# Expert outputs added to a table of sums in DRAM by accumulating indirect transfers

## The chip, the cores and the metric

The kernel runs on one core of a Trainium2 chip. The core has a matrix engine (TensorE, PE in the profile), a vector engine (VectorE, DVE), a scalar engine (ScalarE, ACT), a general engine (GpSimd, POOL) that also issues the indirect transfers, and a queue engine (SyncE, SP) that issues most loads. Sixteen DMA engines move data for all the queues. The metric is the device time of one execution in microseconds (us); less is better.

## The reference, cut to what matters

Two trunk layers run over 640 tokens: 512 latent tokens and 128 context ("prompt") tokens. Each layer ends with an expert-choice mixture of experts. There are 16 experts. Each expert picks its 64 best latent tokens and its 16 best prompt tokens, runs a gated network of width 1024 on these 80 rows, weighs each row by the router's number, and adds it to the row of its token:

```
cap = CAPACITY_FACTOR * n_tok // N_EXPERTS
g, idx = lax.top_k(aff.T, cap)
xe = xt[idx]
hid = jax.nn.silu(jnp.einsum('ecd,edf->ecf', xe, w1)) * jnp.einsum('ecd,edf->ecf', xe, w3)
ye = jnp.einsum('ecf,efd->ecd', hid, w2) * g[..., None].astype(h.dtype)
out = jnp.zeros_like(xt).at[idx.reshape(-1)].add(ye.reshape(-1, D))
...
x = x + gate2 * expert_choice_ffn(h, p['w_router'], p['w_ff1'], p['w_ff3'], p['w_ff2'])
```

The weights are in fp32: three matrices of 1024 x 1024 for each expert, 12 MB. One token can be picked by several experts, so the last line is a sum that several experts write to.

## The kernel before, in words

**State.** The residual stream `x` lies in SBUF with the model dimension on the partitions: 8 tiles of 128 x 640 tokens. Everything that an expert produces has tokens on the partitions, so it has to be spread over tokens and turned before it can be added to `x`.

**A pair of experts.** The experts are worked in 8 pairs (A and B) for each layer. SP streams a pair's weights as 24 chunks of 1 MB into a ring of six buffers (line 705, `ring<-in_w_ff`). It issues a chunk once POOL has counted its buffer free (`chunks_free`, helper `release`). A chunk is two units. For each unit ACT rounds the weights (`w_hi`, `hi_of_chunk`, line 1415), DVE makes the rest (`w_lo`, `lo_of_chunk`, line 1839), and PE multiplies (`job`, line 1361, six matmuls of 512 columns). There are four `w_hi` and four `w_lo` buffers, so ACT and DVE can be four units ahead of PE. A pair has six jobs of eight units: AF0, AF1, BF0, BF1 (hidden halves of A and B), AO and BO (outputs of A and B), 48 units or 288 matmuls. Between them PE turns the hidden values (line 1373) and the next pair's tokens (line 1320), which POOL has fetched from the table `h_rows` in DRAM by indirect transfers (`fetch`, line 770).

**Outputs before.** After job AO, and again after BO, `outputs` of ACT copies the 16 prompt rows from PSUM, makes the rounded and weighed 64 latent rows (`ye_hi`), and issues a store of the prompt rows to DRAM (line 1788). `outputs` of DVE makes the rest (`ye_lo`, line 1847). The latent rows of A lie on partitions 0 to 63 and those of B on 64 to 127; for that B's tokens are padded to 128 rows (`ROWS_OF`, `LAT_OF`). DVE also builds `hot_t`, a 128 x 512 matrix with a one where slot meets token (`place`).

**Combine before.** In the next pair, ahead of each of the eight units 8 to 15 (job AF1), PE multiplies one eighth of `ye_lo` and of `ye_hi` by `hot_t` into a bank of its own (`combine`, line 1331, two matmuls of 512 columns), and DVE adds the result to `x` (`spread`, line 1847). The first pair has nothing to combine. After the last pair the eight combines run by themselves, and then the prompt rows of all 16 experts are read back and multiplied in the same manner (`combine_p`, line 1396), and eight additions end the layer.

**Order.** Each engine's program is written out by hand in this order; engines meet at semaphores. The counts in the loops (`n == 5 + 4 * q`, `n == 21` and so on) say behind which chunk of the pair a step stands on its engine. Pair 0 and the last pair are written out, the six between are a loop.

## Time and profile before

| what | value |
|---|---|
| median of 3 runs | 3278.09 us (3276.85 to 3278.34) |
| the profiled execution | 3273.44 us, its span 3271.7 us |
| granted TensorE clock, mean | 0.948 |
| PE, DVE, ACT, POOL busy | 90%, 65%, 48%, 2% of the span |
| data moved | 566.97 MB, mean 173 GB/s |

All rows quoted below come from one profiled execution, with times in us from the start of its span. "Busy" counts the time in which an engine works on an instruction; matmuls are pipelined, so that one matmul lasts 0.39 us while the next starts 0.23 us after it. The distance from start to start is therefore the better measure of what a matmul costs. The DMA share is the busy share of the 16 DMA engines; it can read a little over 1.

### The profile page before, as it was taken

What the parts mean: (1) busy time and instruction counts of PE and PEld (TensorE: products, weight loads), DVE (VectorE), ACT (ScalarE), POOL (GpSimd) and SP (SyncE); (2) the same over time, 40 slices, a digit from 0 to 9 for tenths busy, and PEclk for the clock granted to TensorE, in tenths of its full rate; (3) what the DMA queues carried; (4) which work ended last, traced back from release to release, by engine and by line L of the source; (5) the groups of instructions that cost most, each with busy time, mean ns of one, the idle gap of its engine ahead of it and who ended that gap; (6) DMA issues with size and microseconds to landing.
All of it is one profiled execution on the core that took longest, in us unless ns stands there. A gap on an engine that the chain in (4) does not pass through costs nothing.

```text
span 3271.7 us, 42479 instructions
## 1 busy us (share of the span) xinstructions
PE 2939.5 (90%) x14740; PEld 2070.8 (63%) x14740; DVE 2114.8 (65%) x3030; ACT 1574.3 (48%) x2328; POOL 58.4 (2%) x86
## 2 busy tenths in 40 slices
PE   5988989999977999999978899889999599999994
PEld 2666755667644776667636677557775366777763
DVE  3274445466445999999844653446662699999994
ACT  3162244124124777777732613431510387777773
POOL 0000000000001000000000000000000000000000
PEclk8998999899987999999989899999999799999996
DMA  7102100310228999999921202020112499999991
GB/s 278 52 33 103 64 27 27 104 67 1 110 77 309 359 345 343 341 338 330 334 84 58 78 34 81 2 104 27 67 39 97 161 361 343 338 344 344 342 338 49
DMA packets 285039, 566.97 MB, mean 173 GB/s; under 512 B 18824, under 2 KB 24672, under 8 KB 284256
## 3 DMA queue, kind: packets, MB, share of 16 engines
q1 hardware_dynamic: 276416, 538.39, 46.3%
q10 hardware_dynamic: 5024, 16.16, 1.3%
q0 software_dynamic: 3456, 10.50, 1.2%
q8 instruction: 92, 1.51, 0.2%
q14 instruction: 51, 0.42, 0.0%
HBM read 548.32 MB, written 16.68 MB: 173 GB/s over the span
## 4 chain that ended last, share of the span: by engine, by line
PE 74%; ACT 8%; DVE 7%; issue 4%; ACTq 3%; DMA 3%; DVEq 1%; POOL 0%; POOLq 0%; SPq 0%
PE mm L1361 24%; PE mm L869 14%; PE mm L827 12%; PE mm L871 4%; DVE w_lo L1839 3%; PE mm L1113 2%; PE mm L899 2%; ACT w_hi L1415 2%; PE oo L1331 2%; ACTq L1787 1%; PE oo L1133 1%; PE tp L1121 1%; PE mm L1201 1%; ACT pt L1415 1%; PE mm L922 1%
## 5 line engine op out<-in xcount | busy, mean ns | idle before, releaser
L1839 DVE TENSOR_TENSOR w_lo<-ring,w_hi 128x1024 fp32r<-128x1024 f32 x768 | 909.7, 1221 | 68.1 <-ACT w_hi L1415 48.7
L1415 ACT ACTIVATE w_hi<-ring 128x1024 fp32r<-128x1024 f32 x768 | 802.7, 1059 | 267.5 <-PE mm L1361 242.7
L1415 ACT ACTIVATE dw_hi<-ring 128x512 fp32r<-128x512 f32 (+1 forms) x168 | 104.9, 627 | 646.6 <-PE mm L871 618.2
L1839 DVE TENSOR_TENSOR dw_lo<-ring,dw_hi 128x512 fp32r<-128x512 f32 (+1 forms) x168 | 115.2, 689 | 399.9 <-ACT dw_hi L1415 399.8
L869 PE MATMUL mm<-h_hi,dw_lo 128*128 128x512 f32 (+1 forms) x672 | 326.4, 486 | 12.1 <-issue 6.2
L871 PEld LDWEIGHTS mm<-h,ring 128*128 128x128 f32 (+1 forms) x1344 | 254.9, 190 | 60.7
L869 PE MATMUL mm<-h_hi,dw_hi 128*128 128x512 f32 (+1 forms) x672 | 268.4, 399 | 0.0
L869 PE MATMUL mm<-h_lo,dw_hi 128*128 128x512 f32 (+1 forms) x672 | 266.5, 397 | 0.0
L827 PE MATMUL mm<-scratch,ring 128*128 128x512 f32 (+1 forms) x896 | 257.9, 440 | 1.6 <-ACT scratch L1415 1.6
L871 PE MATMUL mm<-h,ring 128*128 128x128 f32 (+1 forms) x1344 | 259.1, 274 | 0.0
L827 PEld LDWEIGHTS mm<-scratch,ring 128*128 128x128 f32 x896 | 142.5, 194 | 112.1 <-issue 109.6
L1361 PE MATMUL mm<-w_lo,xa_hi 128*80 128x512 f32 x512 | 204.1, 399 | 9.8 <-DVE w_lo L1839 9.8
L1361 PE MATMUL mm<-w_lo,hid_hi 128*128 128x512 f32 (+1 forms) x512 | 205.9, 402 | 3.2 <-DVE w_lo L1839 2.5
L1361 PE MATMUL mm<-w_lo,xb_hi 128*128 128x512 f32 x512 | 202.5, 396 | 0.0
L1361 PE MATMUL mm<-w_hi,xa_lo 128*80 128x512 f32 x512 | 202.1, 395 | 0.0
L1907 DVE RECIPROCAL tmp<-tmp 128x640 f32<-128x640 f32 x48 | 199.3, 4153 | 3.5
L1361 PE MATMUL mm<-w_hi,hid_lo 128*128 128x512 f32 (+1 forms) x512 | 201.4, 393 | 0.0
L1361 PE MATMUL mm<-w_hi,hid_hi 128*128 128x512 f32 (+1 forms) x512 | 201.0, 393 | 0.0
L1361 PE MATMUL mm<-w_hi,xa_hi 128*80 128x512 f32 x512 | 200.8, 392 | 0.0
L1361 PE MATMUL mm<-w_hi,xb_hi 128*128 128x512 f32 x512 | 199.7, 390 | 0.0
L1361 PE MATMUL mm<-w_hi,xb_lo 128*128 128x512 f32 x512 | 199.3, 389 | 0.0
L1415 ACT ACTIVATE scratch<-mm 128x512 f32<-128x512 f32 (+4 forms) x144 | 97.8, 691 | 158.3 <-PE mm L922 46.3
(255 smaller groups left out, 4631.5 us busy)
## 6 DMA issues: line engine op xcount, KB each, us to landing
ring<-in_w_ff SPq DMA_DIRECT2D x384, 1024.0 KB, 5.9
ring<-in_w_ada SPq DMA_DIRECT2D x48, 1024.0 KB, 7.9
ring<-in_w_gate SPq DMA_DIRECT2D x24, 1024.0 KB, 7.4
ring<-in_w_in SPq DMA_DIRECT2D x16, 1024.0 KB, 10.2
ring<-in_w_o SPq DMA_DIRECT2D x8, 1024.0 KB, 8.7
x_spill<-x ACTq DMA_DIRECT2D x2, 2560.0 KB, 8.6
h_rows<-merged ACTq DMA_DIRECT2D x10, 512.0 KB, 2.7
ring<-in_w_br_da SPq DMA_DIRECT2D x4, 1024.0 KB, 14.2
```

Source lines behind the costliest of these rows:

```text
L827: last = pe.matmul(out[:, lo:hi], lhs(n), rhs(n)[:, lo:hi], start=(n == 0), stop=(n == terms - 1))
L869: pe.matmul(out[0:width, 0:NLAT], w_[u % 2][:, kk, 0:width], h_[:, k, 0:NLAT], start=(k == 0 and i == 0), stop=(k == KT - 1 and i == 2))
L871: last = pe.matmul(out[0:width, NLAT:T], weight(chunk, k, c0, c0 + width), h[:, k, NLAT:T], start=(k == 0), stop=(k == KT - 1))
L899: last = pe.matmul(mm[j % 2][:, 0:width], h[:, k, t * P:(t + 1) * P], weight(chunk, k, c0, c0 + width), start=(k == 0), stop=(k == KT - 1))
L922: last = pe.matmul(mm[turn % 2][32 * kk:32 * kk + 32, 0:512], c_cols[:, half * HALF + kk, :], ring[g % RING][:, kk, :], start=(half == 0), ...
L1113: last = pe.matmul(mm[j % 2][:, at:at + hi - lo], ml_q[hd % 2][:, t * P:(t + 1) * P], ml_k[hd % 2][:, lo:hi], start=True, stop=True)
L1121: last = pe.transpose(tp[:, b * P:(b + 1) * P], ml_p[i % 3][:, b * P:(b + 1) * P], ident)
L1331: last = pe.matmul(oo[j % 2][:, :], y[:, k * P:(k + 1) * P], hot_t[:, :], start=(i == 0), stop=(i == 1))
L1361: last = pe.matmul(out[0:rows_, bank:bank + 512], a_[:, k, 0:rows_], b_[n % SPLITS][:, kk, :], start=(k == 0 and i == 0), stop=(k == KT - ...
L1415: return act.activation(out, in_, ACT.Copy, scale=scale)
L1839: return dve.tensor_tensor(out, in0, in1, op)
L1907: dve.reciprocal(t_[:, :], t_[:, :])
```

## The change

The sum over experts moves from PE and DVE to the DMA engines. Two tables `sums` of 640 x 1024 in DRAM, one for each layer, are set to zero by ten stores early in the first layer (POOL, from a zeroed row tile of `merged`). After AO and after BO, ACT copies all 80 rows of the expert, weighed, from PSUM into a plain fp32 buffer (`ye`), and POOL issues an indirect transfer that adds these 80 rows of 4 KB to the rows of their tokens in `sums` (`add`). The additions are ordered: each waits until the one before it has landed (`added`). They stand behind the release of chunk 22 (for A) and of chunk 3 of the next pair (for B); the token fetches move from chunks 3 and 6 to 4 and 7. At the layer's end ACT waits for the last addition, loads the whole table (2.5 MB) into `merged`, PE turns it in 40 transposes, and DVE adds it to `x` in 16 instructions.

Gone are: `hot_t`, `ye_hi` and `ye_lo`, the combines and their additions, the stores of prompt rows with their read-back and product, the small transfers of `slot_p`, and the padding of B to 128 rows (all jobs now work on 80 rows).

The core of the diff:

```
-PAIR_MM, PAIR_T, PAIR_O = 6, 6, 8
+PAIR_MM, PAIR_T = 6, 6
-        x_hi = [rounded("xa_hi", "scratch", 6144, [P, KT, CAP]), rounded("xb_hi", "scratch", 7424, [P, KT, P])]
+        x_hi = [rounded("xa_hi", "scratch", 6144, [P, KT, CAP]), rounded("xb_hi", "scratch", 7424, [P, KT, CAP])]
-        ye_hi = rounded("ye_hi", "scratch", 11520, [P, D])
-        ye_lo = rounded("ye_lo", "pt", 0, [P, D])
+        ye = [view(11520, D), view(12544, D)]
...
+        def added_count(l, e, half):
+            return 16 * (DEPTH * TT + 2 * l * PAIRS + half) + 32 * e
...  POOL
+            pool.wait_ge(t_full, T_BEFORE)
+            pool.memset(tok[:, 0, :], 0.0).then_inc(zero_ready, 1)
+                if l == 0:
+                    pool.wait_ge(zero_ready, 1)
+                    for n in range(DEPTH):
+                        for t in range(TT):
+                            pool.dma_start(a["sums"][n][t * P:(t + 1) * P, :], tok[:, 0, :]).then_inc(added, 16)
+                def add(of, half):
+                    pool.tensor_copy(row_to[0:CAP, half:half + 1].bitcast(U32),
+                                     row_no[0:CAP, bass.ds(2 * of + half, 1)].bitcast(U32)).then_inc(row_to_ready, 1)
+                    pool.wait_ge(ye_ready, 2 * (l * PAIRS + of) + (half + 1))
+                    pool.wait_ge(added, added_count(l, of, half))
+                    pool.sem_inc(pool_waited, 1)
+                    pool.drain()
+                    pool.indirect_dma_start(a["sums"][l],
+                                            bass.IndirectOffsetOnAxis(ap=row_to[0:CAP, half:half + 1].bitcast(U32), axis=0),
+                                            ye[half][0:CAP, :], None, compute_op=ALU.add).then_inc(added, 16)
+                def pair(e, before=None, last_pair=False):
                     for n in range(PAIR_CHUNKS):
                         release(e, n)
-                        if n in (3, 6):
+                        if n == 3 and before is not None:
+                            add(before, 1)
+                        if n in (4, 7) and not last_pair:
                             ...
                             fetch(e + 1, half)
+                        if n == 22:
+                            add(e, 0)
...  PE
-                        if before is not None and COMBINE_AT <= n < COMBINE_AT + KT:
-                            combine(n - COMBINE_AT, before)
-                                last = pe.matmul(out[0:rows_, bank:bank + 512], a_[:, k, 0:rows_],
+                                last = pe.matmul(out[0:CAP, bank:bank + 512], a_[:, k, 0:CAP],
-                for k in range(KT):
-                    combine(k, PAIRS - 1)
+                pe.wait_ge(ye_back, l * 16 + 16)
+                for k in range(KT):
+                    j = MM["back"] + k
+                    wait_mm_empty(pe, l, j)
+                    for t in range(TT):
+                        last = pe.transpose(mm[j % 2][:, t * P:(t + 1) * P], tok[:, t, k * P:(k + 1) * P], ident)
+                    last.then_inc(mm_full[j % 2], 1)
...  ACT
+                    act.wait_ge(added, added_count(l, e, half) - 16)
+                    copy(ye[half][0:CAP, :], mm[j % 2][0:CAP, :], aff_now[0:CAP, half:half + 1])\
+                        .then_inc(mm_empty[j % 2], 1)
                     act.drain()
-                    act.dma_start(a["ye_pr"][2 * e + half], ye_pr[PR_OF[half], :]).then_inc(ye_stored, 16)
+                    act.sem_inc(ye_ready, 1)
+                act.wait_ge(added, added_count(l, PAIRS, 0))
+                act.dma_start(tok[:, :, :], a["sums"][l].rearrange("(t p) c -> p t c", p=P)).then_inc(ye_back, 16)
...  DVE
+                        if l == 0 and m == 0:
+                            dve.wait_ge(added, 16 * DEPTH * TT)
-                    stt(ye_lo[rows_, :], mm[j % 2][rows_, :], aff_slot[rows_, :], f(ye_hi[rows_, :]),
-                        ALU.mult, ALU.subtract).then_inc(mm_empty[j % 2], 1)
-                            spread(m - SPLITS - COMBINE_AT, before)
+                    j = MM["back"] + k
+                    wait_mm_full(dve, l, j)
+                    for lo, hi, g in groups:
+                        last = stt(x[:, k, lo:hi], mm[j % 2][:, lo:hi], mod[:, 40 + k, g:g + 1], x[:, k, lo:hi],
+                                   ALU.mult, ALU.add)
```

**PE, in the loop over pairs, around units 8 and 9 (job AF1).** Before, two matmuls of the combine stand ahead of each unit (`w_lo_85` and `w_hi_89` are the buffers of unit 8, `oo` the bank of the combine):

```order
2546 L1361 MATMUL mm<-w_hi_92,xa_hi 80x512
2547 L573 ISA
2548 L1331 MATMUL oo<-hot_t,ye_lo 128x512
2549 L1331 MATMUL oo<-hot_t,ye_hi 128x512
2550 L1356 REGISTER_ALU
2551 L1361 MATMUL mm<-w_lo_85,xa_hi 80x512
...
2556 L1361 MATMUL mm<-w_hi_89,xa_hi 80x512
2557 L1331 MATMUL oo<-hot_t,ye_lo 128x512
2558 L1331 MATMUL oo<-hot_t,ye_hi 128x512
```

In the changed kernel the eight pairs of `oo` matmuls are gone, and unit follows unit on the same two banks `mm`.

**PE, at the layer's end.** Before, 16 matmuls of the last combine and 16 of the prompt rows follow the last unit:

```order
3176 L1361 MATMUL mm<-w_hi_92,hid_hi_98 128x512
3177 L1331 MATMUL oo<-hot_t,ye_lo 128x512
...
3192 L1331 MATMUL oo<-hot_t,ye_hi 128x512
3193 L1396 MATMUL mm<-scratch 128x128 x16
3194 L942 MATMUL tp<-const,rows 128x108
```

And in the changed kernel, where 40 transposes of 128 x 128 from the table that was read back (`merged`) take their place:

```order
2846 L1353 MATMUL mm<-w_hi_92,hid_hi_98 80x512
2847 L1383 MATMUL mm<-const,merged 128x128 x40
2848 L948 MATMUL tp<-const,rows 128x108
```

What moved: the sum is no longer formed on PE; what is left there is one turn of the whole table, behind a load.

**POOL, in the loop over pairs.** In the changed kernel (the second number is the line; `sums<-scratch` is an addition, `merged<-h_rows` a fetch, each `REGISTER_ALU` run belongs to the waits and releases of chunks):

```order
25 L774 COPY scratch<-scratch 80x1
26 L776 REGISTER_ALU
27 L777 ISA
28 L780 DMA sums<-scratch 640x1024
...
33 L765 COPY scratch<-scratch 80x1
34 L768 DMA merged<-h_rows,scratch 80x1024
...
38 L765 COPY scratch<-scratch 80x1
39 L768 DMA merged<-h_rows,scratch 80x1024
40 L790 REGISTER_ALU x15
...
45 L780 DMA sums<-scratch 640x1024
```

Before, the loop of this engine held the two fetches alone. Now it holds four indirect transfers for each pair, and the releases of chunks stand behind them in the same queue.

## Rows read from the trace of the kernel before

**Rows 1.** From the page: busy time, share and instructions of each engine.
```profile
PE 2939.5 (90%) x14740; PEld 2070.8 (63%) x14740; DVE 2114.8 (65%) x3030; ACT 1574.3 (48%) x2328; POOL 58.4 (2%) x86
```

**Rows 2.** Windows, core 0: length, busy time by engine, clock, DMA share, GB/s.
```profile
1037.60:1110.10 72.50, 70.83 (x327) 51.28 (x326) 66.34 (x69) 60.61 (x68) 3.63 (x5) 1.00 1.03 365
1186.30:1262.50 76.20, 73.65 (x337) 53.28 (x336) 70.27 (x73) 58.78 (x65) 2.94 (x4) 1.00 0.96 337
```

**Rows 3.** Timeline of PE, starts of units 8 and 16: start, length, instruction.
```profile
1040.02 0.40 PE L1361 MATMUL mm<-w_lo,xa_hi 128*80 128x512 f32 x1
...
1051.35 0.39 PE L1361 MATMUL mm<-w_lo,xb_hi 128*128 128x512 f32 x1
...
1187.52 0.40 PE L1331 MATMUL oo<-hot_t,ye_lo 128*128 128x512 f32 x1
...
1203.60 0.40 PE L1361 MATMUL mm<-w_lo,xb_hi 128*128 128x512 f32 x1
...
1263.73 0.40 PE L1331 MATMUL oo<-hot_t,ye_lo 128*128 128x512 f32 x1
```

**Rows 4.** Timeline of ACT, DVE and PE between two pairs.
```profile
1180.48 1.11 ACT L1415 ACTIVATE ye_hi<-mm,stat 64x1024 fp32r<-64x1024 f32 x1
1182.31 5.08 ACT L1415 ACTIVATE w_hi<-ring 128x1024 fp32r<-128x1024 f32 x5 [0.72 <-issue]
1183.40 6.91 DVE L1839 TENSOR_TENSOR w_lo<-ring,w_hi 128x1024 fp32r<-128x1024 f32 x6 [0.49 <-ACT w_hi L1415]
1184.68 0.46 PE L1361 MATMUL mm<-w_lo,xa_hi 128*80 128x512 f32 x1 [0.70 <-DVE w_lo L1839]
```

**Rows 5.** Timeline of PE: each third matmul of B's input, then of A's output.
```profile
1222.82 0.39 PE L1361 MATMUL mm<-w_lo,xb_hi 128*128 128x512 f32 x1
...
1225.54 0.39 PE L1361 MATMUL mm<-w_lo,xb_hi 128*128 128x512 f32 x1
...
1226.93 0.39 PE L1361 MATMUL mm<-w_lo,hid_hi 128*80 128x512 f32 x1
...
1229.73 0.39 PE L1361 MATMUL mm<-w_lo,hid_hi 128*80 128x512 f32 x1
```

**Rows 6.** The same for 10 us at full rate, and 10 with fetches.
```profile
1060.00:1070.00 10.00, 10.00 (x48) 8.26 (x47) 9.60 (x12) 8.05 (x9) 0.00 (x0) 1.00 1.05 386
1270.00:1280.00 10.00, 10.00 (x48) 6.86 (x47) 9.98 (x13) 5.68 (x7) 1.30 (x2) 1.00 1.05 336
```

**Rows 7.** DMA issues: out and in, queue, count, KB each, median us to landing.
```profile
ring<-in_w_ff SPq DMA_DIRECT2D x384, 1024.0 KB, 5.9
x_spill<-x ACTq DMA_DIRECT2D x2, 2560.0 KB, 8.6
merged<-h_rows,scratch POOLq DMA_INDIRECT x32, 7.5
```

**Rows 8.** Timeline of POOL and PE: the second fetch, one under load, turns.
```profile
1022.98 0.92 POOL L770 DMA_INDIRECT merged<-h_rows,scratch  x1 [2.27 <-issue]
1026.92 1.30 PE L1320 MATMUL tp<-const,merged 80*128 80x80 f32 x8 [3.34 <-DMA merged<-h_rows,scratch]
1187.83 1.00 POOL L770 DMA_INDIRECT merged<-h_rows,scratch  x1 [0.89 <-issue]
1235.62 0.74 PE L1320 MATMUL tp<-const,merged 80*128 80x80 f32 x8 [0.40 <-DVE hid_lo L1839]
```

**Rows 9.** Timeline of the first layer's end, and a turn of eight tiles.
```profile
966.37 1.97 PE L1302 MATMUL tp<-const,h 128*128 128x128 f32 x8 [0.97 <-DVE scratch L2289]
1630.29 0.39 PE L1361 MATMUL mm<-w_hi,hid_hi 128*128 128x512 f32 x1
1640.75 1.41 DVE L1847 SCALAR_TENSOR_TENSOR x<-oo,mod,x 128x512 f32<-128x512 f32 x2 [0.16 <-PE oo L1331]
1646.15 2.16 DVE L1847 SCALAR_TENSOR_TENSOR x<-mm,mod,x 128x128 f32<-128x128 f32 x8 [3.99 <-PE mm L1396]
```

**Rows 10.** Windows: a stretch of attention in the first layer.
```profile
180.00:200.00 20.00, 13.33 (x68) 8.26 (x69) 12.74 (x33) 8.99 (x21) 0.00 (x0) 0.74 0.10 35
```

More of the change, by code:

```diff
@@ L199 @@
     ("pairs", 0)])
-MM["combine_p"] = _mm_dense + PAIRS * PAIR_MM
-MM_LAYER = MM["combine_p"] + 1
+MM["back"] = _mm_dense + PAIRS * PAIR_MM
+MM_LAYER = MM["back"] + KT
 MM_USES = [(MM_LAYER + 1) // 2, MM_LAYER // 2]
@@ L266 @@
 TOKENS_AT = (38, 42)
-COMBINE_AT = JOB_UNITS
 def job_turn(q):
@@ L803, in _ @@
                             fetch(e + 1, half)
-                for n in range(PAIR_CHUNKS):
-                    release(PAIRS - 1, n)
+                        if n == 22:
+                            add(e, 0)
+                pair(0)
+                with pool.Fori(1, PAIRS - 1) as e:
+                    pair(e, e - 1)
+                pair(PAIRS - 1, PAIRS - 2, True)
+                add(PAIRS - 1, 1)
         @block.tensor
@@ L1322, in turn_tokens, with job @@
                     last.then_inc(t_full, 1)
-                def combine(k, of):
-                    if k == 0:
-                        pe.wait_ge(ye_done, l * PAIRS + of + 1)
-                    j = OO["pairs"] + k
-                    wait_o_empty(pe, l, j, of)
-                    for i, y in enumerate((ye_lo, ye_hi)):
-                        last = pe.matmul(oo[j % 2][:, :], y[:, k * P:(k + 1) * P], hot_t[:, :],
-                                         start=(i == 0), stop=(i == 1))
-                    last.then_inc(o_full[j % 2], 1)
-                def job(q, e, before=None, last_pair=False):
+                def job(q, e, last_pair=False):
                     half = q % 2 if q >= AO else q // 2
-                    rows_ = ROWS_OF[half]
                     hi, lo = (hid_hi[half], hid_lo[half]) if q >= AO else (x_hi[half], x_lo[half])
@@ L2310, in _ @@
                 dve.tensor_copy(row_no[0:CAP, :].bitcast(U32), tp[0:CAP, 0:NE]).then_inc(slots_ready, 1)
[L2311 to L2317 removed]
+                dve.tensor_copy(slot_aff[0:CAP, :], tp[0:CAP, NE:2 * NE]).then_inc(t_empty, 1)
                 dve.drain()
@@ L2401, in pair @@
                         if n == 14:
-                            place(e)
-                        if n == 21:
-                            if not last_pair:
-                                lo_of_tokens(0, e + 1)
-                            outputs(AO, e)
+                            weigh(e)
+                        if n == 21 and not last_pair:
+                            lo_of_tokens(0, e + 1)
                         if n == 23 and not last_pair:
@@ L2413, in _ @@
                     lo_of_tokens(half, 0)
-                pair(0)
-                place_prompt()
-                with dve.Fori(1, PAIRS - 1) as e:
-                    pair(e, e - 1)
-                pair(PAIRS - 1, PAIRS - 2, True)
-                outputs(BO, PAIRS - 1)
-                for k in range(KT):
-                    spread(k, PAIRS - 1)
-                dve.drain()
-                j = MM["combine_p"]
-                wait_mm_full(dve, l, j)
-                for k in range(KT):
-                    stt(x[:, k, NLAT:T], mm[j % 2][:, k * P:(k + 1) * P], mod[:, 40 + k, 1:2], x[:, k, NLAT:T],
-                        ALU.mult, ALU.add)
-                dve.drain()
-                for s in (mm_empty[j % 2], x_ready, layer_free):
+                with dve.Fori(0, PAIRS - 1) as e:
+                    pair(e)
+                pair(PAIRS - 1, True)
+                for k in range(KT):
+                    j = MM["back"] + k
[3 more added lines that the diff above has]
+                                   ALU.mult, ALU.add)
+                    last.then_inc(mm_empty[j % 2], 1)
+                dve.drain()
+                for s in (x_ready, layer_free):
                     dve.sem_inc(s, 1)
@@ L2469 @@
     a["h_rows"] = nc.dram_tensor("h_rows", (T, D), FP32, kind="Internal").ap()
-    a["slot_p"] = nc.dram_tensor("slot_p", (2, SLOTS_P), FP32, kind="Internal").ap()
-    a["ye_pr"] = nc.dram_tensor("ye_pr_rows", (NE, CAP_P, D), FP32, kind="Internal").ap()
+    a["sums"] = [nc.dram_tensor(f"sums{n}", (T, D), FP32, kind="Internal").ap() for n in range(DEPTH)]
     build(nc, a)
```

151 lines of the change are left out of this document (35 added, 116 removed).

## The prediction

> **What bounds the kernel now.** I read the page first. PE is busy for 90% of the span, DVE for 65% and POOL for 2% [rows 1]. The change touches the expert stages, so I then asked for windows of one pair each. A pair in the loop lasts 76.2 us. PE is busy for 73.65 of them at clock 1.00, DVE for 70.3 and ACT for 58.8, and the DMA share is 0.96 at 337 GB/s [rows 2]. So three resources are close together, and PE is the one that paces: its matmuls follow each other at 0.23 us and it waits little. Third I read the timelines of PE: where the combines stand, what happens between two pairs, and what a matmul on 80 rows costs [rows 3 to 5]. Fourth, since the change gives work to the DMA engines, I looked for their ceiling. There are windows of 10 us at 386 GB/s with the share at 1.05 [rows 6]. Last I read the end of the layer, where PE and DVE finish what the stage left over [rows 9].
>
> **PE in the stage: less by 32.6 us a layer.** Three terms.
> - The combines. Pair 0 has none: its units 8 to 15 take from 1040.02 to 1051.35, 11.33 us. In a pair that has them the same units take from 1187.52 to 1203.60, 16.08 us [rows 3]. That is 4.75 us for 16 matmuls of 0.23 (3.7) and the stalls on the two `oo` banks. Seven pairs of a layer have them: 33.3 us. The eighth set stands in the tail, below.
> - The boundary. ACT makes the prompt copy and `ye_hi`, issues a store, and resumes `w_hi` at 1182.31; DVE resumes `w_lo` at 1183.40, and PE waits 0.70 us for it [rows 4]. Afterwards one copy of 80 x 1024 (like the 1.11 us of `ye_hi`) and no `ye_lo` stand there, so both resume more than 1 us sooner and the wait goes: 7 x 0.7 = 4.9 us.
> - The padding of B. Matmuls on 128 rows start 2.72 us apart for twelve, those on 80 rows 2.80 for twelve [rows 5]. In a pair 96 input matmuls of B and 48 output matmuls go from 128 rows to 80. The output ones cost 4 x 0.08 = 0.3 us by these rows. Units 8 to 15 of pair 0, on 80 rows, took 11.33 us for 48 matmuls and four small transposes (0.2), so 0.231 each against 0.227: 0.4 us for 96. I take 0.7 us a pair, which costs 8 x 0.7 = 5.6 us. Fewer rows save nothing, because 512 columns stream either way.
>
> Sum: -33.3 - 4.9 + 5.6 = -32.6 us a layer. If PE still paces, the stage that ended at 1630.5 [rows 9] ends at 1597.9, and a pair lasts about 71.5 us. DVE loses its additions and `ye_lo` (some 8 us of a pair) and ACT a copy, so neither takes PE's place.
>
> **DMA in the stage: does it still keep up?** This decides the case. At 386 GB/s a chunk of 1.049 MB takes 2.72 us. From the first free buffer (a ring of six is full at the start) 186 chunks have to come: 505 us. A fetch moves 0.33 MB, 0.85 us at that rate; but with fetches in flight the share stays 1.05 and the rate falls to 336 GB/s, which costs 10 x 50 / 386 = 1.3 us more [rows 6]; I take 2.0 us each, 14 of them: 28 us. With the small stores the need is 536 us. By the other measure, share over the saturated 1.05, the stage of 602 us needs 0.91 of itself, 550 us [rows 2]; the share overstates a queue that isn't full. I take 540, of which 2.5 go with the stores of prompt rows.
>
> An addition appears in no row. Bounds: 0.85 us if it costs no more than its bytes, and 15 us if each DMA engine takes its 5 rows one after the other and is held for 3 us by each, which is what an unloaded fetch takes from the end of its issue to its landing (1022.98 + 0.92 to 1026.92) [rows 8]. The nearest row is the fetch, 2.0 us, to which an addition adds one more passage over the same bytes (read the table, read `ye`, write the table): 2.0 + 0.85 = 2.85 us. Fifteen of them before the last chunk: 43 us.
>
> The last chunk then lands at 1029 + 537.5 + 43 = 1609.5, and after it come one `w_hi` (1.1), one `w_lo` (1.2) and two units of six matmuls (2.8): 1614.6. That is later than PE's 1597.9, so the DMA engines pace the stage. It ends 16 us sooner than before, and not 33.
>
> The Trainium skill ("DMA: Bandwidth & Descriptors", section Specifications) speaks against the change: HBM gives one core about 358 GB/s. The trace has stretches of 386 GB/s [rows 6], so the rule doesn't hold for this kernel as it runs; taken literally it would make the chunks alone last 545 us and the changed stage end some 40 us later than in my sum.
>
> **POOL.** Its queue holds the releases of chunks. An addition costs it a small copy, a drain of 0.9 us and 1.0 us of issue [rows 8], 2.5 us in all, and the next release is due 2.8 us later: it fits. The wait for `ye_ready` is over before it is asked, since ACT makes the copy ahead of the `w_hi` on which the release of chunk 22, or chunk 3, depends. The wait for the addition before is over if that landed within the five chunks (14 us) between; fetches land in 7.5 [rows 7]. Were it late, chunks behind it would be released late, and SP would wait: that is part of rival 2. The zeroing writes 5.2 MB (14 us at full rate) where the DMA share is 0.10, long before `merged` is written [rows 10]: nothing. The iota, the `slot_p` transfers and the small DVE copies ahead of the stage: -0.3 us.
>
> **The tail: more by about 10.5 us a layer.** Before, from the last matmul's start at 1630.29 to the end of the last addition at 1648.31 [rows 9]: 17.8 us after the product is there. Now: ACT's copy 1.1 and drain 0.2; POOL 1.0 and issue; landing about 4.5 from the issue's start (the unloaded fetch: 3.9); then the load of 2.5 MB, 8.6 as the spill of the same size [rows 7]. PE starts at about +15.2. A transpose of 128 x 128 takes 1.97 / 8 = 0.246 us [rows 9], 40 of them 9.85; DVE works beside them (0.71 + 0.27 = 0.98 for each five) and ends 1.2 later. PE has been idle for 15 us, and the trace shows what that does: the same eight small transposes take 1.30 us when PE was idle ahead of them and 0.74 in the stream [rows 8]; I add 2 us for it. Sum 28.3, more by 10.5. Bounds: +7 (landing 3, clock back at once) to +20 (the addition lands in 14 us).
>
> **Sum.** Per layer -16 + 10.5 = -5.5 and the small -0.3, so -11.6 for two. The profiled execution took 3273.4 us (span 3271.7), so 3261.8; the median of the runs stands 4.7 above the profiled one: 3266.5.
>
> **Rivals.**
> 1. PE still paces, because an addition costs 1.7 us or less. For: additions are spread thinly, and in rows 2 the rate of 365 GB/s was held over a whole pair. Against: a fetch already costs 2.0. Per layer -32.6 + 10.5 - 0.3 = -22.4: 3233 us.
> 2. Slower: an addition costs more than a plain transfer, because each row is read, added and written back by an engine that the weight loads need. The loss begins at 537.5 + 15c + 5.1 + 1029.3 + 10.2 = 1630.5, which is c = 3.2 us. At 5 us the two layers lose 2 x 15 x 1.8 = 54: 3332. At 15 us, 3632. For: nothing hides it, the DMA share is already 0.96. Against: only the bound from serial rows makes it dear.
> 3. The stage gains what I say, but the gain and the tail cancel (c of 2.9 to 3.3, or a landing of 14 us): 3272 to 3284.
> 4. The change does what it says only on paper: POOL falls behind and holds the releases. Each late release costs its lateness; 2 us a pair make 32 us: about 3300. For: four indirect transfers a pair in the queue that frees the ring; against: the 2.8 us between releases.
> 5. Memory as a whole caps the rate, reads and writes together, at the 365 GB/s that pair 0 kept up as its mean [rows 2]. A chunk then takes 2.87 us, 28 us more for 186: 3323. Against: 386 GB/s for 10 us at a time [rows 6]. The skill's 358 GB/s is a rule of this kind; it has its chance here.
>
> **Chances.** Forecast (DMA paces, additions 1.7 to 2.9 us, 3233 to 3271): 0.36. Rival 1: 0.17. Rival 3: 0.14. Rival 2: 0.23. Rival 4: 0.07. Rival 5: 0.03. Within 0.2% (6.6 us), about what a measurement of this kernel can tell, lies rival 3. Faster: 0.36 + 0.17 = 0.53; same 0.14; slower 0.33. The forecast's own range is 3233 to 3271; my value of an addition lies at its upper end. The range that should hold 8 in 10 reaches to rival 1 on one side and to an addition of 5 us on the other: 3230 to 3332.
>
> **What would show it.** Right: the pairs last 73 to 75 us, all alike but for the first; ACT's `w_hi` waits for the landing of `ring<-in_w_ff`, the median landing of which rises from 5.9 us to over 9; the share is 1.03 or more through the stage; the last matmul to the end of the layer takes about 28 us. PE pacing would show as pairs of 71.5 us and `w_hi` waiting for PE. Rival 2: pairs over 76 us with GB/s below 340 at full share. Rival 4: SP waits for POOL while POOL waits for `sums<-scratch`. I am wrong as a whole if units 8 to 15 don't shrink to 11.3 us, or if the tail grows by less than 5 or more than 20 us.

## The result, and the profile after

| | median | runs | ratio to before |
|---|---|---|---|
| before, on the same chip | 3277.47 us (3275.89 to 3278.34) | 4 | |
| changed | 3226.28 us (3223.72 to 3226.98) | 4 | 0.984, 95% interval 0.983 to 0.986 |

I predicted 3267 us, within 3230 to 3332. The kernel became 51 us faster and the time lies below the range. What came out is rival 1: PE still paces, 3233 us by its sum. The profiled execution took 3226.98 us, its span 3225.1 us, 46.6 us less than before.

The page after, to be held against [rows 1]: PE lost 58 us of work and POOL gained 102.

```profile
PE 2881.5 (89%) x14500; PEld 1938.4 (60%) x14500; DVE 1993.6 (62%) x2820; ACT 1531.8 (47%) x2264; POOL 160.8 (5%) x147
```

Windows of the changed kernel (length, busy time by engine, clock, DMA share, GB/s), for [rows 2]. Each has the length of one pair: the first begins in the third pair of layer one, the other at the end of the fifth.

```profile
1187.53:1257.40 69.87, 69.23 (x321) 44.62 (x320) 62.67 (x60) 56.65 (x62) 10.21 (x9) 1.00 1.05 375
1382.09:1452.69 70.60, 69.38 (x322) 44.49 (x321) 62.18 (x60) 55.69 (x61) 10.07 (x8) 1.00 1.05 375
```

From first matmul to first matmul, the second and third pair last 69.9 us and the later ones 70.4 to 70.6, where it was 76.2. PE is busy for all but 0.6 us of the early stretch. The share is 1.05, that of the windows at full rate in [rows 6].

Starts of units 0, 8, 16, 32 and of the next pair's unit 0 on PE, for [rows 3]. Before, unit 8 started with a combine and unit 16 came 16.08 us later.

```profile
1176.74 0.39 PE L1353 MATMUL mm<-w_lo,xa_hi 128*80 128x512 f32 x1
...
1187.77 0.40 PE L1353 MATMUL mm<-w_lo,xa_hi 128*80 128x512 f32 x1
...
1199.12 0.40 PE L1353 MATMUL mm<-w_lo,xb_hi 128*80 128x512 f32 x1
...
1221.83 0.40 PE L1353 MATMUL mm<-w_lo,hid_hi 128*80 128x512 f32 x1
...
1246.61 0.39 PE L1353 MATMUL mm<-w_lo,xa_hi 128*80 128x512 f32 x1
```

And those of the kernel before that [rows 3] don't have: unit 0, B's input to its end, and the pair's end.

```profile
1175.54 0.40 PE L1361 MATMUL mm<-w_lo,xa_hi 128*80 128x512 f32 x1
...
1226.22 0.40 PE L1361 MATMUL mm<-w_lo,hid_hi 128*80 128x512 f32 x1
...
1251.77 0.40 PE L1361 MATMUL mm<-w_lo,xa_hi 128*80 128x512 f32 x1
```

Unit 0 to 8 took 11.98 us and takes 11.03; units 8 to 15 took 16.08 and take 11.35. Job B's input, 96 matmuls, takes 22.71 us on 80 rows and took 22.62 on 128 (from 1203.60). The two output jobs took 25.55 and take 24.78. The boundary between the pairs on ACT and DVE, for [rows 4]: one copy, then `w_hi` again, and no wait of PE.

```profile
1180.66 1.10 ACT L1401 ACTIVATE scratch<-mm,scratch 80x1024 f32<-80x1024 f32 x1
1181.99 3.00 ACT L1401 ACTIVATE w_hi<-ring 128x1024 fp32r<-128x1024 f32 x3 [0.23 <-issue]
...
1183.09 7.20 DVE L1819 TENSOR_TENSOR w_lo<-ring,w_hi 128x1024 fp32r<-128x1024 f32 x6 [1.07 <-ACT w_hi L1401]
```

POOL in the fifth pair (start, length, instruction, idle before). The addition of the pair before (1327.79) is followed by a fetch, and between the fetch's small copy and its issue POOL stands idle for 5.5 us:

```profile
1327.79 1.51 POOL L780 DMA_INDIRECT sums<-scratch  x1 [0.91 <-issue]
1328.83 1.75 POOL L765 COPY scratch<-scratch 80x1 uint32 x1
1336.12 1.07 POOL L768 DMA_INDIRECT merged<-h_rows,scratch  x1 [5.54 <-issue]
```

What ACT waited for from 1311.45 to 1382.09, a pair's length (engine, operand, line, releaser: us in total, times, longest):

```profile
ACT w_hi L1401 <- PE mm L1353: 8.0, 20, 1.6
ACT w_hi L1401 <- DMA ring<-in_w_ff: 6.3, 9, 1.4
```

DMA queues in three windows of 10 us of the changed kernel (queue, packets, MB, busy share of the 16 engines): one with nothing but chunks, one with a single addition, one with a single fetch. q1 are the chunks, q0 POOL's transfers.

```profile
q1 hardware_dynamic: 1938, 3.87, 105.2%
...
q1 hardware_dynamic: 1674, 3.33, 89.0%
q0 software_dynamic: 96, 0.33, 16.4%
...
q1 hardware_dynamic: 1682, 3.35, 94.1%
q0 software_dynamic: 96, 0.33, 10.9%
```

An addition takes 0.54 MB of chunks away from its window, which is 1.40 us at 387 GB/s. A fetch takes 0.52 MB, 1.34 us. The other windows of this kind in the stage read the same: 3.32 or 3.33 MB of chunks beside nearly every addition, 3.33 to 3.38 beside most fetches.

The start of a stage, for [rows 8]: the second fetch is issued at 1026.77 and PE turns its rows at 1033.95, 7.2 us later; before it was 3.9.

```profile
1026.77 0.95 POOL L768 DMA_INDIRECT merged<-h_rows,scratch  x1 [3.76 <-issue]
...
1033.95 1.30 PE L1326 MATMUL tp<-const,merged 80*128 80x80 f32 x8 [6.96 <-DMA merged<-h_rows,scratch]
```

The end of the first layer, for [rows 9]: an addition, the last matmul, the last addition, the load of the table, the turns, and DVE's last group of additions into `x`.

```profile
1593.30 1.55 POOL L780 DMA_INDIRECT sums<-scratch  x1 [0.86 <-issue]
...
1596.35 0.39 PE L1353 MATMUL mm<-w_hi,hid_hi 128*80 128x512 f32 x1
...
1601.74 1.43 POOL L780 DMA_INDIRECT sums<-scratch  x1 [6.70 <-DMA sums<-scratch]
...
1609.19 0.39 ACTq L1801 DMA_DIRECT2D merged<-sums  x1
...
1618.20 5.63 PE L1383 MATMUL mm<-const,merged 128*128 128x128 f32 x25 [21.47 <-DMA merged<-sums]
...
1622.01 5.82 DVE L1827 SCALAR_TENSOR_TENSOR x<-mm,mod,x 128x512 f32<-128x512 f32 x12 [0.36 <-PE mm L1383]
```

From the last matmul's start to the end (1627.83) it is 31.5 us, before 18.0. In layer two it is 27.1 us against 17.6. There the last addition is issued 2.9 us after the last matmul's start, and not 5.4, and it lands in 5.2 us (the load is issued at 3158.49), and not in 7.5. What differs is the traffic beside it. In layer one SP has already issued six loads of 1 MB for the next layer (`ring<-in_w_in`, from 1585.47 on), and the last layer has no next one. The addition in layer two, and the two stretches from issue to landing, layer one first (the two last columns are DMA share and GB/s):

```profile
3153.31 1.43 POOL L780 DMA_INDIRECT sums<-scratch  x1 [4.21 <-DMA sums<-scratch]
```

```profile
1601.74:1609.19 7.45, 0.00 (x0) 0.00 (x0) 0.00 (x0) 0.00 (x0) 1.43 (x1) 0.50 0.89 293
3153.31:3158.49 5.18, 0.00 (x0) 0.00 (x0) 0.00 (x0) 0.00 (x0) 1.43 (x1) 0.72 0.46 63
```

So the span's 46.6 us are: the two stages, first matmul to start of the last, -41.0 and -40.9; the two ends +13.5 and +9.5; from the first fetch's issue to the stage's first matmul +3.9 and +3.1 (9.83 to 13.70 us, 13.36 to 16.45). That is -51.9. The rest, +5.3, lies in the dense parts; +3.2 of it is there when the first fetch is issued, and executions of the changed kernel differ by 2.4 us at that point.

### The profile page after: what moved, and what is told of

Its sections match the earlier page's. It is cut to its first block, busy times and chain, and to the rows that moved or that the text cites. A ratio compares the mean times of both kernels' runs of the same rounds, so it can differ in the third digit from the quotient of the medians.

```text
span 3225.1 us, 41854 instructions
## 1 busy us (share of the span) xinstructions
PE 2881.5 (89%) x14500; PEld 1938.4 (60%) x14500; DVE 1993.6 (62%) x2820; ACT 1531.8 (47%) x2264; POOL 160.8 (5%) x147
## 4 chain that ended last, share of the span: by engine, by line
PE 70%; DMA 10%; DVE 6%; issue 6%; ACT 5%; ACTq 1%; POOLq 1%; DVEq 1%; POOL 0%; SPq 0%
PE mm L1353 19%; PE mm L875 15%; PE mm L833 12%; DMA ring<-in_w_ff 6%; PE mm L877 5%; PE mm L1119 2%; PE mm L905 2%; DVE w_lo L1819 2%; ACT w_hi L1401 1%; PE oo L1139 1%; PE tp L1127 1%; PE mm L1207 1%; PE mm L1010 1%; PE mm L928 1%; PE tp L1219 1%
## 5 line engine op out<-in xcount | busy, mean ns | idle before, releaser
L1353 PE MATMUL mm<-w_lo,hid_hi 128*80 128x512 f32 x512 | 204.3, 399 | 0.0
L1353 PE MATMUL mm<-w_lo,xb_hi 128*80 128x512 f32 x512 | 203.0, 396 | 0.0
L1353 PE MATMUL mm<-w_hi,hid_hi 128*80 128x512 f32 x512 | 202.3, 395 | 0.0
L1353 PE MATMUL mm<-w_hi,hid_lo 128*80 128x512 f32 x512 | 202.3, 395 | 0.0
L1353 PE MATMUL mm<-w_hi,xb_lo 128*80 128x512 f32 x512 | 201.7, 394 | 0.0
L1353 PE MATMUL mm<-w_hi,xb_hi 128*80 128x512 f32 x512 | 200.2, 391 | 0.0
L875 PEld LDWEIGHTS mm<-h_hi,dw_hi 128*128 128x128 f32 (+1 forms) x672 | 128.0, 190 | 30.0
```

Source lines behind the costliest of these rows:

```text
L875: pe.matmul(out[0:width, 0:NLAT], w_[u % 2][:, kk, 0:width], h_[:, k, 0:NLAT], start=(k == 0 and i == 0), stop=(k == KT - 1 and i == 2))
L1353: last = pe.matmul(out[0:CAP, bank:bank + 512], a_[:, k, 0:CAP], b_[n % SPLITS][:, kk, :], start=(k == 0 and i == 0), stop=(k == KT - 1 an ...
```

## The experiments

All are compared with the kernel before on their own chip, whose median was 3276.7 to 3278.1 in the four sets of runs. "Stage" is the first layer's, from its first matmul to the start of its last: 602.3 us before, 561.4 in the changed kernel. Its end is counted from there to DVE's last addition.

### 1. No additions

```
-                            add(before, 1)
...
-                            add(e, 0)
...
-                act.wait_ge(added, added_count(l, PAIRS, 0))
+                act.wait_ge(added, 16 * DEPTH * TT)
```

> The changed kernel with all 32 additions left out (the table stays zero, so the experts' outputs do not reach the result), and with the waits for them. Theory A (PE paces the changed stage, the DMA engines only just keep up): pairs of 69.5 to 70.6 us, at most 1 us less than the 70.6 of the changed kernel, so the two stages shrink by 0 to 16 us in all; the end of the layer loses the landing of the last two additions, some 12 us a layer. Time 3185 to 3204. Theory B, the step of my prediction (the DMA engines pace the changed stage and an addition costs them 2.85 us): 15 of them come before the last chunk of a stage, so the stage would fall by 43 us until PE holds it; PE was then faster than I counted, pairs of about 66 us and a time near 3130.

Measured: 3202.46 us, ratio 0.977 (0.976 to 0.979). Stage 558.6 us. Theory A holds: 16 additions cost the stage 2.8 us in all. Theory B is dead. Of the 24 us between this kernel and the changed one, 15 lie at the layers' ends, where two landings are gone (23.5 us for 31.5, and 20.4 for 27.1; I had expected 12 a layer), and 6 in the two stages. A stretch of one pair's length:

```profile
1258.72:1328.56 69.84, 69.20 (x321) 44.63 (x320) 62.66 (x60) 56.63 (x62) 4.23 (x5) 1.00 1.04 370
```

PE has 69.20 of 69.84 us, so this is PE's own pace.

### 2. Two more additions in each pair, and six

```
+                        if n in (11, 15) and before is not None:
+                            i = (11, 15).index(n)
+                            again(before, i % 2, i // 2)
```

`again` issues the same transfer into a further table (`sums_x`), behind a wait for the last one into that table and a drain of its own. There are two such tables, taken in turn.

> The changed kernel with two more additions in each pair but the first, of the same rows into two further tables, between chunks 11 and 15, where the POOL queue is free. The profile of the changed kernel shows 1.64 us of the 16 engines for the packets of one addition. Theory A (the engines are full at 1.05 in the changed stage, an addition costs 1.6 us of them): pairs go from 70.6 to 73 to 74 us, 14 x 2.4 to 3.4 = 34 to 48 us more in all: 3260 to 3275. Theory B (2.85 us each): 14 x 5.7 = 80 us more: 3306. Theory C (there is slack, PE alone paces): pairs stay under 71.5, 3226 to 3240.

> The same with six more additions in each pair but the first, at chunks 9, 11, 13, 15, 17 and 19. Against the kernel with two more, the slope gives the price of one without regard to who paces at the start: 4 x 14 = 56 additions. Theory A, 1.64 us each: 92 us over the kernel with two more, pairs of 80 us. Theory B, 2.85 us: 160 us over it, pairs of 85 us. Rival: the POOL queue, which an addition holds for some 2 us, comes to hold the releases of chunks; then SP waits for POOL and the DMA share falls below 1.0.

Measured with two more: 3261.06 us, ratio 0.996 (0.994 to 0.997), stage 579.5. That is 18.1 us for 14 additions in the stage, 1.3 each: theory A, whose 1.6 is the nearer value. With six more: 3536.36 us, ratio 1.079 (1.077 to 1.081), stage 722.4. That is 143 us for 28 further ones, 5.1 each, and 275 us in both layers, where theory A had 92 and theory B 160: the rival took over. A stretch of one pair's length, what SP waited for in it, and POOL's transfers:

```profile
1289.87:1382.53 92.66, 74.63 (x321) 47.01 (x320) 62.43 (x60) 55.90 (x62) 17.40 (x14) 0.89 0.94 307
```

```profile
SPq L697 <- POOLq L804: 79.6, 14, 8.8
```

```profile
1340.86 1.68 POOL L793 DMA_INDIRECT sums_x<-scratch  x1 [7.35 <-DVE w_lo L1836]
1350.61 1.41 POOL L793 DMA_INDIRECT sums_x<-scratch  x1 [8.06 <-issue]
```

The share falls to 0.94 and the rate to 307 GB/s: the DMA engines have room and don't get the work. SP waits for POOL for 79.6 us of 92.7. POOL brings out one indirect transfer in about 9 us, since the drain ahead of each waits for the one before; ten of them are the pair's 92.7 us. This is rival 4 of the prediction. It bounds a pair with eight additions, and not yet one with four.

### 3. Is it the adding? Plain writes

```
-                                            ye[half][0:CAP, :], None, compute_op=ALU.add).then_inc(added, 16)
+                                            ye[half][0:CAP, :], None).then_inc(added, 16)
```

> The changed kernel with its 32 transfers into the table as plain indirect writes instead of additions (a row then holds only the last expert's output). Theory A (adding costs the DMA engines more than writing, since the row of the table is read too): the packets of one transfer fall from the 1.64 us of 16 engines that the profile of the changed kernel shows to the 1.1 us of a fetch, ACT waits less for the chunks, pairs of 70.0 instead of 70.6 us, time 8 to 12 us less: 3214 to 3218. Theory B (the price is that of the packets' way, not of the adding): 1.64 us as before, no change: 3226. In both the landing of the last two stays near 7.5 us.

Measured: 3211.79 us, ratio 0.980 (0.978 to 0.982). Theory A, a little more than it said. A window of 10 us with one write in it, to be held against the one with an addition above:

```profile
q1 hardware_dynamic: 1799, 3.59, 96.8%
q0 software_dynamic: 96, 0.33, 8.2%
```

A write occupies the 16 engines for 8.2% of 10 us, an addition for 16.4%: 0.82 and 1.64 us, exactly twice. It takes 0.28 MB of chunks away, 0.7 us, half of an addition's 1.4. The stage is 558.7 us and ACT waits for no chunk. The last transfer also lands sooner, which neither theory had: in 5.3 us instead of 7.5, in layer two in 3.3 instead of 5.2. The end is 28.0 instead of 31.5 us, in layer two 24.7 instead of 27.1.

### 4. POOL's hold, or the DMA engines? One addition moved

```
-                        if n == 3 and before is not None:
+                        if n == 12 and before is not None:
                             add(before, 1)
```

> The changed kernel with the addition of the pair before's second half (BO) issued behind chunk 12 and not behind chunk 3. In the changed kernel the fetch behind chunk 4 follows that addition, and POOL's drain ahead of it waits 5.6 us, in which no release of a chunk can go out; ACT then waits for ring<-in_w_ff. Theory A (the 0.3 us a pair that the kernel without additions was faster come from POOL's hold): the wait goes, pairs shrink from 70.2 to 69.9, 5 us less in all: 3221. Theory B (they come from the engines' own work for an addition, twice that of a plain write): no change, 3226.

> The changed kernel itself, unchanged, for a comparison on the same chip with the two others: 3226, between 3222 and 3229.

Measured: 3218.24 us moved, ratio 0.9825 (0.9812 to 0.9839), and 3221.56 us for the changed kernel again, 0.9833 (0.9819 to 0.9846), a little below the 3222 to 3229 that I had said. The two medians differ by 3.3 us and the intervals overlap, so by the times it is a hint. The stages are clearer: 558.7 against 561.5, and 557.8 against 560.8 in layer two. ACT's waits in four pairs, of the changed kernel again and then of the moved one:

```profile
ACT w_hi L1401 <- DMA ring<-in_w_ff: 17.8, 28, 2.2
```

```profile
ACT w_hi L1401 <- PE mm L1353: 51.7, 141, 1.3
```

The waits for chunks, 17.8 us in four pairs, are gone at the same share and the same GB/s:

```profile
1312.40:1382.27 69.87, 69.23 (x322) 44.62 (x321) 62.67 (x60) 56.64 (x61) 10.04 (x9) 1.00 1.05 375
```

So what the additions cost the stage came from their place behind chunk 3, right ahead of a fetch, as theory A said. But experiment 3 removed it too, with a cheaper transfer left in that place. Neither theory alone is the cause; the next run shows why.

### 5. Two more additions, without the hold

Experiment 2's two with experiment 4's move, at chunks 15 and 18.

> Two more additions in each pair but the first, as in the kernel with two more, but with POOL's transfers spread so that each drain finds the one before it nearly done: fetches behind chunks 4 and 7, additions behind 12, 15, 18 and 22. Theory A (an addition slows the stage through POOL's hold of the releases, and the DMA engines have room for it): the stage stays at 559 to 563 us, against 579 with the two more at chunks 11 and 15 and the other behind chunk 3; time near 3220. Theory B (the DMA engines have no room left, their packets of 1.64 us for an addition are the price): 14 more of them make the stage 14 x 1.2 to 1.6 = 17 to 23 us longer, 576 to 582; time 3253 to 3264.

Measured: 3254.61 us, ratio 0.993 (0.991 to 0.995). Stage 575.9 us, 17.2 more than without them, 1.2 each: theory B, and POOL's hold is not the price. Its pairs last 71.8 and 74.9 us in turn from the fourth on, 73.3 in the mean. A stretch of that length:

```profile
1429.46:1502.76 73.30, 70.63 (x326) 45.05 (x325) 62.24 (x59) 56.05 (x63) 11.65 (x11) 1.00 1.05 370
```

Both hang together by this sum. A pair needs of the DMA engines 24 chunks of 1.049 MB at 387 GB/s, 65.1 us, and two fetches and two additions, 2.7 + 2.8: 70.6 us. Four additions make it 73.4, and the mean pair lasts 73.3. PE needs 69.85. So the changed kernel is just past the point where they meet. What hides it is a reserve, since the six buffers are full when the stage starts. By this sum seven pairs of experiment 5 lose 7 x 3.55 = 25 us, and the stage lost 17, so the reserve is worth some 8 us, an estimate. Seven pairs that each lose 0.7 us use up 5 of them: hidden, as long as no hold of the releases takes the reserve first. A cheaper transfer or a kinder place are each enough.

### 6. What the combines cost

In the kernel before, the 16 combining matmuls of a pair and DVE's 8 additions left out, their semaphores kept:

```
-                        last = pe.matmul(oo[j % 2][:, :], y[:, k * P:(k + 1) * P], hot_t[:, :],
-                                         start=(i == 0), stop=(i == 1))
-                    last.then_inc(o_full[j % 2], 1)
+                    pe.sem_inc(o_full[j % 2], 1)
```

> The kernel before with the 16 combining matmuls of each pair and the 8 additions into x on DVE left out (only their semaphores pass), so the latent rows miss the experts' sum. My term: 4.75 us a pair less on PE, 7 pairs and the 8th set in the tail, 2 x (33.3 + 4.7) = 76 us less, pairs of 71.5 us: 3201. Rival: what is left of the boundary and the 128 rows keep PE longer, or DMA at 386 GB/s holds it (24 chunks of 2.72 us and two fetches are 67.7 us): pairs of 72 to 74.

Measured: 3229.72 us, ratio 0.986 (0.985 to 0.988), stage 578.2, pairs of 72.76, so 29 us more than I had said. The pairs shrink by 3.44 us, not by 4.75. A wait of PE in the first part of a pair:

```profile
1187.87 0.45 PE L1358 MATMUL mm<-w_lo,xa_hi 128*80 128x512 f32 x1 [1.14 <-DVEq L2338]
```

It costs 1.3 us (1.53 us from the start of the matmul ahead instead of 0.23) and is one that the experiment kept: PE waits for the semaphore that DVE passes on in place of its addition, and DVE is late there. The kernel before has that wait too, for DVE's `x`:

```profile
1192.06 0.50 PE L1331 MATMUL oo<-hot_t,ye_lo 128*128 128x512 f32 x1 [0.71 <-DVE x L1847]
```

With it the sum is 3.44 + 1.3 = 4.74 us, the size of my term; that the wait goes with the combines is argued, since no run takes it out alone. The changed kernel has no such wait, and its pairs are 2.9 us shorter than these.

The eighth set, at the layer's end, was worth nothing, where I had 4.7 us. The end takes 20.9 us without it and 18.0 with it. PE there waits for the prompt rows to be read back, and the combines had stood in that wait. Without them PE is idle for 11.8 us, and the product of the prompt rows behind it takes 6.48 us at a granted clock of 0.57, a mean of both levels, where it took 3.84 at 1.00 (2.4 GHz).

### 7. The second fetch: what follows it on POOL

```
                 fetch(0, 1)
+                kick(0)
```

and `kick` behind each of the last two additions too. In one kernel it is `pool.dma_start(a["kick"][...], const[0:1, 0:P])`, in the other `pool.drain()`.

> The changed kernel with a small plain transfer (512 bytes) issued by POOL right behind the second fetch of a stage and behind each of the last two additions. In the kernel before, other POOL transfers stood behind the second fetch and it landed 3.9 us after its issue; in the changed kernel it stands alone and takes 7.2. Theory A (an indirect transfer gets going sooner when the POOL queue has another transfer behind it): it lands after some 4 us, and so do the last two additions; 3 x 3.3 us less a layer, 20 us in all: 3206. Theory B (the 7.2 us has another cause): no change, 3226, or 1 to 2 us more from the three issues.

> The same three places with a drain of the POOL queue in place of the small transfer. In the changed kernel the drain behind the first fetch of a stage waits 3.8 us, that behind an addition or a fetch in the loop 5.5 to 6.8 us, about as long as the transfer's packets take to start. Theory A' (any POOL instruction that waits for the engine makes the descriptors come sooner than an idle wait on a semaphore): fetch and additions land after some 4 to 5 us, up to 15 us less in all. Theory B' (the drain only waits for what takes 7 us anyway): no change, 3226.

Measured: small transfer 3224.00 us, ratio 0.984 (0.982 to 0.985); drain 3220.49 us, ratio 0.982 (0.981 to 0.984). The second fetch's issue and its turn, first with the small transfer, then with the drain:

```profile
1024.61 0.95 POOL L773 DMA_INDIRECT merged<-h_rows,scratch  x1 [3.87 <-issue]
...
1031.40 1.30 PE L1335 MATMUL tp<-const,merged 80*128 80x80 f32 x8 [6.59 <-DMA merged<-h_rows,scratch]
```

```profile
1026.37 0.95 POOL L771 DMA_INDIRECT merged<-h_rows,scratch  x1 [3.88 <-issue]
...
1030.28 1.30 PE L1333 MATMUL tp<-const,merged 80*128 80x80 f32 x8 [3.69 <-DMA merged<-h_rows,scratch]
```

6.8 us and 3.9 us. Theory A of the small transfer falls; the drain gives the 3.9 us of the kernel before, in both layers (4.0 in the second). What makes the difference stands on SP's queue. The first two chunks that it issues as buffers come free, in the changed kernel and then with the drain:

```profile
1026.61 0.92 SPq L696 DMA_DIRECT2D ring<-in_w_ff  x2
```

```profile
1030.34 0.92 SPq L696 DMA_DIRECT2D ring<-in_w_ff  x2
```

In the changed kernel POOL releases the first buffers right behind the fetch, and two chunks of 1 MB go out together with it. The DMA share is 1.04 at 403 GB/s two microseconds later, and the fetch's packets move 4.5 to 6.5 us after its issue. The drain holds those releases back until the fetch has landed. Its packets then have the engines to themselves and move 1.5 to 3.5 us after its issue. The other two kernels fit: with the small transfer the chunks go out at 1024.92, together with the fetch, and in the kernel before, where two stores and a wait for their landing held POOL, at 1029.27, after it had landed. The second layer shows the same (chunks at 2580.64 beside a fetch at 2580.80, and at 2581.01 behind one at 2576.93). No run holds the releases back by a plain wait alone; the kernel before comes nearest to that.

Behind the last additions no release is waiting, and there the drain did nothing: in layer one the second went out 8.7 us after the first, before 8.4, and the end took 32.0 us.

### 8. The table by row tiles

```
-                act.dma_start(tok[:, :, :], a["sums"][l].rearrange("(t p) c -> p t c", p=P)).then_inc(ye_back, 16)
+                for t in range(TT):
+                    act.dma_start(tok[:, t, :], a["sums"][l][t * P:(t + 1) * P, :]).then_inc(ye_back[t], 16)
```

PE and DVE then go through the tiles in that order.

> The changed kernel with the table loaded in five transfers of 128 rows, each with its own semaphore, and turned and added row tile by row tile (8 transposes and 8 additions of 128 columns each) instead of column block by column block. The load of 2.5 MB takes 9.0 us; now PE starts after the first fifth. DVE has 40 additions of 0.27 us, 10.8 us, the first after some 4 us. The end of the layer: 18.6 us from the load's issue to the last addition become 14 to 15, 4 us less a layer: 3216 to 3220. Rival: five smaller transfers are slower to land, or DVE's 40 short instructions cost more than 0.3 us each: no gain.

Measured: 3220.41 us, ratio 0.982 (0.981 to 0.984). First turn 3.3 us after the load's issue and not 9.0; then DVE paces:

```profile
1609.14 2.38 ACTq L1802 DMA_DIRECT2D merged<-sums  x5
...
1612.47 1.94 PE L1383 MATMUL mm<-const,merged 128*128 128x128 f32 x8 [15.68 <-DMA merged<-sums]
...
1614.45 10.43 DVE L1828 SCALAR_TENSOR_TENSOR x<-mm,mod,x 128x128 f32<-128x128 f32 x40 [20.86 <-PE mm L1383]
```

The end takes 28.5 us instead of 31.5, in layer two 24.2 instead of 27.1: 3 us a layer, where I had said 4.

### 9. All together

The drain behind the second fetch, the row tiles, the move, and in the last pair the first addition behind chunk 21, with each addition's drain ahead of its waits.

> The version the runs point to: the changed kernel with a drain behind the second fetch of a stage (that fetch then lands in 3.9 instead of 7.2 us: 3.3 us a layer), the table loaded and turned by row tiles (2.9 us a layer), the last pair's first addition behind chunk 21 instead of 22 and the drain of an addition ahead of its waits (2 to 3.5 us a layer), and the addition behind chunk 12 as above. Sum if they add up: 8 to 10 us a layer, 3206 to 3210. Rival: the last addition waits for its product anyway, and the moves at the stage's end give nothing: 3213.

Measured: 3204.21 us (3201.41 to 3204.44, 5 runs), ratio 0.978 (0.977 to 0.979), 17.4 us less than the changed kernel in the same set of runs, and 2 us below my range. Stage 558.5, its end 26.8 us, in layer two 23.2. The last addition now waits for nothing but ACT's copy, 0.9 us behind it:

```profile
1590.34 1.41 POOL L780 DMA_INDIRECT sums<-scratch  x1 [4.98 <-ACTq L1769]
```

## Why the prediction was wrong

- **The step that failed** is "DMA in the stage", and in it the price of an addition. It took 2.85 us of the DMA engines, and so made them end after PE. The displaced chunks show 1.40 us. With this one value changed, my own sum has the last unit end at 1029.3 + 537.5 + 15 x 1.40 + 5.1 = 1592.9, ahead of PE's 1597.9, and PE's end stands. Experiments 1 and 5 show it from both sides: without additions the stage is 2.8 us shorter, with 14 more it is 17.2 longer.
- **The rest of the need was too high as well.** 186 chunks of 2.71 us (504), 14 fetches of 1.34 (19) and the additions (20) are 543 us, where I had 537.5 + 43 = 580.5. By the order on POOL 14 additions stand ahead of the last chunk, not 15.
- **How the sizes went wrong.** For the addition I took the fetch and added a passage. By the queue's busy share adding is twice a plain write (1.64 and 0.82 us), but a plain write is cheaper than a fetch (1.09), so the sum of a fetch and a passage was too much. The fetch's 2.0 us was not far off for the kernel it was read from: beside single fetches, the windows at full share in the loop of the kernel before have 3.0 to 3.2 MB of chunks against 3.84 without one, 1.6 to 2.1 us. Only pair 0, which has no combines, shows a value like that of the changed kernel (3.32 MB, 1.34 us). What makes a fetch cheaper there is not shown. The 540 was a mean of two estimates, of which one took fetches at 2.0 us and the other a share over 1.05.
- **The forecast's place in the range.** I had c of 1.7 as rival 1's condition and gave it 0.17. The value that the runs show, 1.40, lies nearer to my lower bound of 0.85 than to the 2.85 that I chose, and that choice decided the case.
- **PE, right in kind, a quarter too small.** Forecast with PE pacing: 4.7 us less a pair, 71.5 us; PE's own pace is 69.87, 6.3 less. Units 8 to 15: 4.75 us predicted, 4.73 measured. The boundary: 0.7 predicted, 0.95 measured (11.98 to 11.03). The padding of B, a loss of 0.7 predicted: the 96 input matmuls lost 0.1 (22.62 to 22.71), and the output jobs gained 0.77 (25.55 to 24.78) where I had a loss of 0.3. I had said in one clause that DVE gets 8 us back and not asked what PE gains by it: in the output jobs its waits for DVE's `w_lo`, `hid_lo` and `xa_lo` fell from 1.2 to 0.6 us.
- **POOL, right with a wrong detail.** It does not hold PE. But an addition is not "2.5 us and it fits": the drain of the next transfer waits 5.5 us or more, and costs about 3 us a stage where a fetch follows an addition (experiment 4). At ten transfers a pair it is the bound (experiment 2).
- **The tail: +10.5 predicted, +13.5 and +9.5 measured**, within its bounds, but partly by errors that cancel. The load came later in layer one: the last addition was issued 5.0 us after the product was there, where I had 2.3, since it waited for the one before to land, and it landed in 7.5 us and not 4.5, with the next layer's loads beside it. In layer two, without them, it was 2.5 and 5.2 us. The turns were cheaper: 9.6 us from the first turn to DVE's end, where I had 13. DVE paced them (1.4 us to its start, 7.9 us of work, 0.4 idle).
- **The clock was counted twice.** I took a turn at 0.246 us from eight that ran at a granted clock of 0.50, the lower level of 1.2 GHz (966.30 to 968.40), and added 2 us for PE's idle time on top. After the wait the turns here ran at 0.50 too, 0.21 us apart, and from 1623 on at 1.00 (2.4 GHz), five in 0.76 us:

```profile
1618.20:1620.60 2.40, 2.40 (x10) 2.00 (x10) 1.01 (x2) 0.00 (x0) 0.00 (x0) 0.50 0.00 0
1624.14:1624.90 0.76, 0.76 (x5) 0.52 (x5) 0.76 (x2) 0.00 (x0) 0.00 (x0) 1.00 0.00 0
```

The lower clock cost about 1 us of the end, an estimate: DVE started after five turns in 1.37 us instead of 0.76, and stood idle for 0.4 later.
- **The start of the stage: -0.3 predicted, +3.9 and +3.1 measured.** I counted the `slot_p` transfers as work to be saved. They stood between the second fetch and the first releases, and without them the first chunks run beside the fetch, which lands 3.3 us later (experiment 7).
- **The HBM rule.** The Trainium skill ("DMA: Bandwidth & Descriptors", Specifications) has about 358 GB/s for one core. The changed kernel keeps 375 over a pair's length and 387 between transfers, so the rule failed here. Another page of the Trainium skill, "Perfetto Trace Analysis", section Engine Utilization, says that 358 is the share when both cores of a pair are active and that one core alone can draw more, up to some 435. This trace agrees with that one.

## What to carry to other kernels

To price a transfer that runs beside a saturated stream, compare two equal windows, one with it and one without, and take the bytes that the stream lost; then check the sum against the slack of the engine that paces, because a few tenths of a microsecond per period decide who paces. A chain at the end of a stage (last product, transfer, wait for the transfer before, load back, turn) is not thinned by any of this: it costs its full length, and is best cut by loading back in pieces and issuing the next-to-last transfer as early as it can go. When small transfers are removed from a queue that also releases buffers, look at what they held back: the loads released sooner share the DMA engines with a transfer that somebody waits for.

## What the runs showed of the hardware that I had not expected

- An accumulating indirect transfer of 80 rows of 4 KB occupies the 16 DMA engines for 1.64 us, the plain write 0.82 us, the gather 1.09 us (16.4%, 8.2% and 10.9% of 10 us). The stream beside it loses 1.40, 0.7 and 1.34 us in the changed kernel.
- POOL's drain behind an indirect transfer waits for it: 3.8 us with the DMA engines idle, 5.5 to 8 beside the chunks. Ten such transfers filled a pair of 92.7 us, about 9 us each, with the engines at a share of 0.94.
- How soon an indirect transfer lands goes by what the DMA engines carry beside it. A fetch took 3.9 us from its issue with nothing beside it and 7.2 beside two chunks, an addition 5.2 and 7.5 us, a plain write 3.3 and 5.3. The Trainium skill ("DMA: Bandwidth & Descriptors", Anatomy of one DMA) fits 2.0 us plus the bytes over 436 GB/s to a transfer of this kind, an estimate of 2.75 us for these 0.33 MB. No indirect transfer whose landing was read here came in so soon; the nearest is the write in layer two, 3.3 us.
